# The second output product in two halves: the convolution's columns beside the recurrence's output stage

## The reference

```
y, ... = rwkv_bidir(...)                              # the recurrence
yn  = (y - mean) * rsqrt(var + eps) * gn_g + gn_b     # per head of 64
a_x = (yn + bonus) * (sigmoid(xg) @ g_up)
b_x = short_conv(px_cv, conv_w)
x   = x + g1 * (concatenate([a_x, b_x]) @ w_out)      # 1024 x 1024 weights
hx  = modulate(rmsnorm(x, norm2_g), sh2, sc2)
x   = x + g2 * expert_choice_ffn(hx, router_w, ...)
```

## Time and profile before

| | us |
|---|---|
| runs | 2788.32, 2792.85, 2795.87 |
| median | 2792.85 |
| the profiled execution | 2790.04 |
| its span in the trace | 2788.0 |
| recurrence's chunks | 1414 to 1907 |
| recurrence's output | 1908 to 1969 |
| output product with scores | 1969 to 2109 |
| TensorE busy, share of the span | 2370.7, 85% |
| VectorE busy, share of the span | 1687.5, 61% |

### The profile page before, as it was taken

How to read it: one execution, slowest core, us unless ns; L and a number is a source line. 1 busy time by engine, 2 the same in 40 slices (tenths; PEclk the granted TensorE clock), 3 DMA queues, 4 the chain that set the end, 5 groups by cost and what they waited for, 6 DMA issues and landing times. The chain is left out here.

```text
span 2788.0 us, 55283 instructions
## 1 busy us (share of the span) xinstructions
PE 2370.7 (85%) x23038; PEld 1852.1 (66%) x23038; DVE 1687.5 (61%) x2124; ACT 980.6 (35%) x1536; POOL 665.8 (24%) x672
## 2 busy tenths in 40 slices
PE   4998988899987599997858888888691799999994
PEld 2876755578866488886237777775481588888883
DVE  5981569421143655664645555553447899999994
ACT  3112532311032400000424333333220577777773
POOL 1321676123300123220045555440000000000000
PEclk8999999999998599997579999997795799999997
DMA  5331024411132453110321101101532599999994
GB/s 214 113 106 63 1 82 121 168 31 46 31 122 105 133 192 118 39 38 12 127 86 27 31 22 26 26 12 51 221 112 107 227 407 407 393 395 397 398 384 171
DMA packets 135851, 401.45 MB, mean 144 GB/s; under 512 B 55410, under 2 KB 65266, under 8 KB 108114
## 3 DMA queue, kind: packets, MB, share of 16 engines
q1 hardware_dynamic: 124692, 363.70, 35.1%
q0 software_dynamic: 4608, 16.78, 2.5%
q10 hardware_dynamic: 6336, 17.80, 1.7%
HBM read 342.64 MB, written 55.59 MB: 143 GB/s over the span
## 5 line engine op out<-in xcount | busy, mean ns | idle before, releaser
L3336 DVE TENSOR_TENSOR ex_wl<-ew_raw,ex_wh 128x2048 fp32r<-128x2048 f32 x192 | 435.4, 2289 | 41.9 <-ACT ex_wh L3298 38.3
L3298 ACT ACTIVATE ex_wh<-ew_raw 128x2048 fp32r<-128x2048 f32 x192 | 367.5, 1919 | 108.7 <-PE ex_U L3242 40.3
L130 PE MATMUL sp_acc<-b2h_hi,sp_wh 128*128 128x512 f32 (+1 forms) x528 | 194.8, 369 | 12.9 <-POOL sp_wl L1710 12.9
L130 PE MATMUL sp_acc<-b2h_lo,sp_wh 128*128 128x512 f32 (+1 forms) x528 | 194.4, 368 | 0.0
L130 PE MATMUL sp_acc<-b2h_hi,sp_wl 128*128 128x512 f32 (+1 forms) x528 | 194.3, 368 | 0.0
L3219 POOL DMA_INDIRECT x<-ex_o,ex_at x16 | 26.5, 1657 | 494.6 <-DVE ex_o L3359 494.6
L2361 DVE TENSOR_TENSOR rc_t<-rc_chain,b_level 128x256 f32<-128x256 f32 x200 | 84.5, 423 | 85.3 <-PE rc_chain L2459 83.5
L1708 POOL CAST sp_wh<-sp_w 128x1024 fp32r<-128x1024 f32 x26 | 27.8, 1069 | 409.4 <-DMA sp_w<-in_w_conv 233.5
L130 PEld LDWEIGHTS sp_acc<-b2h_hi,sp_wh 128*128 128x128 f32 x528 | 100.1, 190 | 30.6 <-POOL sp_wl L1710 13.3
L130 PEld LDWEIGHTS sp_acc<-b2h_hi,sp_wl 128*128 128x128 f32 x528 | 100.0, 189 | 16.6
L130 PEld LDWEIGHTS sp_acc<-b2h_lo,sp_wh 128*128 128x128 f32 x528 | 100.2, 190 | 16.3
(11 more groups left out here) (485 smaller groups left out, 6062.1 us busy)
## 6 DMA issues: line engine op xcount, KB each, us to landing
ew_raw<-in_exp_gate SPq DMA_DIRECT2D x64, 1024.0 KB, 7.8
ew_raw<-in_exp_up SPq DMA_DIRECT2D x64, 1024.0 KB, 8.9
ew_raw<-in_exp_down SPq DMA_DIRECT2D x64, 1024.0 KB, 7.4
b2p_pT<-in_ada_w SPq DMA_DIRECT2D x32, 512.0 KB, 6.2
rc_ac<-ac SPq DMA_DIRECT2D x40, 256.0 KB, 3.6
b_pj<-in_ada_w SPq DMA_DIRECT2D x8, 1024.0 KB, 11.9
ssm_wm<-in_w_merge SPq DMA_DIRECT2D x16, 512.0 KB, 3.6
ac<-rp_ac SPq DMA_DIRECT2D x4, 2048.0 KB, 7.2
```

The source lines that it names most:

```text
L130: ins = nc.tensor.matmul(out, w[a][:, k, :], h[b][:, k, cols], start=(first and n == 0), stop=(last and n == 2))
L3298: nc.scalar.activation(wh[:, n % RING], raw[:, n % RING], ACT.Copy).then_inc(q["w_hi"], 1)
L3336: V.tensor_tensor(wl[:, n % RING], raw[:, n % RING], wh[:, n % RING].bitcast(f32), ALU.subtract).then_inc(q["w_lo"], 1)
```

## The change

The rows 4 to 7 of w_out and the columns b_x are multiplied in the output stage of the recurrence, and their part is added to the residual on chip; the later stage multiplies only a_x, which stays in SBUF.

- `rwkv_chunks` gets a function `ahead`, by which SP loads w_out's rows 4 to 7 (512 KB each) before the loop.
- `rwkv_output` loads b_x (in four pairs of blocks), the row g1, the residual `xm` and w_out's rows 0 to 3. ScalarE and VectorE split the weights (`weight_high`, `weight_low`) and columns (`columns_high`, `columns_low`); TensorE has 16 units `product(b, h)` of 12 matmuls between its other work; ScalarE evacuates each unit, and GpSimd multiplies by g1 and adds to `xm`, two passes per block. The fan, the gate and the sums have one PSUM buffer each. The result is not stored. The split weights lie over the inputs of the recurrence.
- `out_scored` has four k instead of eight: 24 matmuls per block, scores before k = 1, transpositions before k = 3, no loads of weights, columns or residual. It stands inside the phase `b2p`, which owns semaphores now.
- The recorded offset of a tile is rounded up to 32 bytes.

```diff
@@ rwkv_chunks, SP
                 sp.dma_start(ka[:, 0], I["kcols"][:, 1, :]).then_inc(ka_loaded, 16)
+                ahead(sp)
@@ rwkv_output, GpSimd and SP
+                for b in range(NB):
+                    t = tmp[:, b % 2, :]
+                    pool.wait_ge(q["evacuated"], 2 * b + 2)
+                    nc.gpsimd.tensor_tensor(t, t, row[:], ALU.mult).then_inc(q["weighed"], 1)
+                    pool.wait_ge(q["weighed"], b + 1)
+                    pool.wait_ge(xm_loaded, 32)
+                    nc.gpsimd.tensor_tensor(xm[:, b, :], xm[:, b, :], t, ALU.add).then_inc(q["xm_ready"], 1)
...
-                    sp.dma_start(aT_dram[:, b, hs], bonus[:, b, hs]).then_inc(q["stored"], 16)
+                for i in range(4):
+                    sp.wait_ge(q["w_lo"], i + 1)
+                    sp.dma_start(ow[:, i, :], I["w_out2"][:, i, :]).then_inc(ow_loaded[i], 16)
@@ rwkv_output, TensorE (fanned(n) waits for scaled >= n, gated(n) for done >= n)
+                def product(b, h):
+                    u = 2 * b + h
+                    pe.wait_ge(q["s_lo"], b + 1)
+                    if u >= 3:
+                        pe.wait_ge(q["evacuated"], u - 2)
+                    for k in range(4):
+                        if u == 0:
+                            pe.wait_ge(q["w_lo"], k + 1)
+                        nc.tensor.matmul(prod[:, u % 3, :], sh[:, b % 2, k, :], wh[:, 4 + k, halves[h]], start=(k == 0), stop=False)
+                        nc.tensor.matmul(prod[:, u % 3, :], sh[:, b % 2, k, :], wl[:, 4 + k, halves[h]], start=False, stop=False)
+                        last = nc.tensor.matmul(prod[:, u % 3, :], sl[:, b % 2, k, :], wh[:, 4 + k, halves[h]], start=False, stop=(k == 3))
...
+                product(3, 0)
+                fanned(3)
+                gated(3)
+                summed(7)
+                product(3, 1)
                 turned(1)
                 for n in range(4, N):
+                    product(n // 2 + 2, n % 2)
                     fanned(n)
                     gated(n)
+                for b in (6, 7):
+                    for h in range(2):
+                        product(b, h)
@@ rwkv_output, ScalarE
+                for b in range(1, NB):
+                    if b + 1 < NB:
+                        columns_high(b + 1)
+                    evacuate(2 * b)
+                    if b == 1:
+                        unit(4)
+                    if b == 2:
+                        unit(6)
+                    evacuate(2 * b + 1)
...
+                    if b < HP:
+                        biased(b)
+                    if b == 3:
+                        rooted(1)
+                    if 2 <= b < 6:
+                        weight_high(2 + b)
@@ rwkv_output, VectorE
                 meaned(0)
...
+                output(1)
+                weight_low(4)
+                output(2)
+                columns_low(4)
+                output(3)
                 meaned(1)
+                weight_low(5)
+                columns_low(5)
+                weight_low(6)
+                output(4)
+                columns_low(6)
+                output(5)
+                weight_low(7)
+                columns_low(7)
+                output(6)
+                output(7)
@@ out_scored
+    KA = 4
...
-                    for k in range(KD):
-                        if k == 2 and b >= 2:
+                    for k in range(KA):
+                        if k == 1 and b >= 2:
                             scored(b - 2)
-                        if k == 6 and b >= 1:
+                        if k == 3 and b >= 1:
                             turned(b - 1)
...
-                    V.tensor_tensor(yb, yb, xt[:, s, :], ALU.add).then_inc(q["added"], 1)
+                    V.tensor_tensor(yb, yb, xm[:, b, :], ALU.add).then_inc(q["added"], 1)
```

More of the change, by code:

```diff
@@ L2625, in _, with rwkv_output @@
                 outputs(NCK, (NCK - 1) % 2)
-def rwkv_output(nc, T, I, pT, y, bonus_dram, bonus, aT_dram):
+def rwkv_output(nc, T, I, pT, y, bonus_dram, bonus, bx_dram, xmid, mod_dram, split, ow, ow_loaded, xm, row):
+    wh, wl = split
+    halves = [slice(0, 512), slice(512, 1024)]
     with Phase(nc, "ro") as ph:
@@ L2682, in turned @@
                     for i in range(4):
-                        last = nc.tensor.transpose(var[0:8, h, i * P:(i + 1) * P], inv[:, h, i * 8:(i + 1) * 8], T.ident[:])
+                        last = nc.tensor.transpose(var[0:8, i * P:(i + 1) * P], inv[:, h, i * 8:(i + 1) * 8], T.ident[:])
                     last.then_inc(q["turned"], 1)
[L2686 to L2691, removed]
                 def fanned(n):
@@ L2695, in fanned @@
                     pe.wait_ge(q["rows_ready"], h + 1)
-                    if n >= 2:
-                        pe.wait_ge(q["scaled"], n - 1)
-                    nc.tensor.matmul(fan[:, n % 2, :], heads[:, b, :], inv_rows[:, h, :], start=True, stop=True).then_inc(q["fanned"], 1)
+                    if n == 0:
+                        pe.wait_ge(q["loaded"], 48)
+                    else:
+                        pe.wait_ge(q["scaled"], n)
+                    nc.tensor.matmul(fan[:], heads[:, b, :], inv_rows[:, h, :], start=True, stop=True).then_inc(q["fanned"], 1)
@@ new lines, in gated @@
+                def gated(n):
+                    h, b = todo[n]
+                    if n:
+                        pe.wait_ge(q["done"], n)
+                    nc.tensor.matmul(gate[:], gup[:, b * P:(b + 1) * P], pT[:, XB, CTX + h * 512:CTX + (h + 1) * 512], start=True, stop=True).then_inc(q["gated"], 1)
+                def product(b, h):
[9 more added lines that the diff above has]
+                        last = nc.tensor.matmul(prod[:, u % 3, :], sl[:, b % 2, k, :], wh[:, 4 + k, halves[h]], start=False, stop=(k == 3))
+                    last.then_inc(q["product"], 1)
@@ L2701, in _ @@
                 pe.wait_ge(q["matrix"], 1)
                 centred(0)
[L2703 to L2706, removed]
+                centred(1)
+                summed(0)
+                centred(2)
+                summed(1)
+                product(0, 0)
+                centred(3)
+                summed(2)
+                product(0, 1)
+                summed(3)
+                product(1, 0)
@@ L2707, in _ @@
+                turned(0)
+                centred(4)
+                product(1, 1)
+                fanned(0)
                 gated(0)
+                summed(4)
+                centred(5)
+                product(2, 0)
+                fanned(1)
                 gated(1)
[L2709 to L2716, removed]
+                summed(5)
@@ L2717, in _ @@
+                centred(6)
+                product(2, 1)
+                fanned(2)
+                gated(2)
+                summed(6)
+                centred(7)
+                product(3, 0)
[3 more added lines that the diff above has]
+                product(3, 1)
                 turned(1)
                 for n in range(4, N):
+                    product(n // 2 + 2, n % 2)
                     fanned(n)
                     gated(n)
+                for b in (6, 7):
+                    for h in range(2):
+                        product(b, h)
@@ L2740, in biased @@
                         act.wait_ge(q["loaded"], 48)
-                    nc.scalar.activation(bonus[:, b, :], bonus[:, b, :], ACT.Identity, bias=cols[:, 1, b:b + 1]).then_inc(q["biased"], 1)
-                for n in range(4):
-                    unit(n)
-                biased(0)
[L2746 to L2751, removed]
+                    A(bonus[:, b, :], bonus[:, b, :], ACT.Identity, bias=cols[:, 1, b:b + 1]).then_inc(q["biased"], 1)
@@ new lines, in evacuate @@
+                def evacuate(u):
+                    b, h = u // 2, u % 2
+                    act.wait_ge(q["product"], u + 1)
+                    if b >= 2 and h == 0:
+                        act.wait_ge(q["xm_ready"], b - 1)
+                    A(tmp[:, b % 2, halves[h]], prod[:, u % 3, :], ACT.Copy).then_inc(q["evacuated"], 1)
+                weight_high(0)
+                unit(0)
+                weight_high(1)
+                columns_high(0)
+                unit(1)
+                weight_high(2)
```

184 lines of the change are left out of this document (98 added, 86 removed).

## The result

The changed kernel runs 2806.61 us (median, 2799.87 to 2809.83), beside 2793.24 for the kernel before: ratio 1.0042, 95% interval 1.0023 to 1.0061 (the ratio is estimated over all runs; that of the two medians is 1.0048). The profiled execution of the first comparison, 2799.87 us with a span of 2798.1, is the quickest of its four runs.

What follows compares the result with a forecast made beforehand. It took the product's stage as bound by TensorE, after 14 us of loading, and the output stage as holding little work. +47.7 - 48.5 + 4.5 + 3.1 + 0.9 = +7.7 gave 2797.7, as a median 2800; range 2782 to 2818.

Steps and rivals of the forecast that it cites:

- TensorE's work and its waits: Output stage: 74.9 us of TensorE work at full clock, plus waits from the new order, tail and stage change, 98.3.
- D: Output stage: fan 7, behind unit 11, waits for weight-low 7 and columns-low 7; 4.95 us.
- B: Output stage: second transposition waits for unit 7, its evacuation, a bias, a square root and reciprocal; 2.55 us.
- C: Output stage: fan 5 waits for output 4 behind weight-low 6, and gate 5 waits too; 4.35 us.
- The clock in the output stage: Half clock on TensorE after idle time, a little more than one stretch: 5 us, bounds 0 and 15.
- A: Output stage: fan 3 waits for output 2's scaling, which stands behind weight-low 4 on VectorE; 3.3 us.
- The product's stage: Later stage: no load in front, blocks 9.7 us apart on VectorE's chain; -48.5 us, and +4.5 for half clock.
- The chunk loop's start: Four weight rows issued in front of the loop's first transfers delay its start; +3.1 us, bounds 0 and 6.
- The extra barrier: Leaving the enclosing phase, which now owns semaphores, costs one more change of stage; +0.9 us.
- rival 2: Product's stage loses the clock in every block, at idle time before the transposes: 15 instead of 4.5, 2811; chance 0.17.
- 1: Rival: clock holds in both stages and GpSimd seldom meets VectorE on a path; 2780 to 2791, say 2786; chance 0.30.
- 3: Rival: output stage stays at half clock throughout; about +40, 2840; chance 0.08.

Runs made afterwards that it cites:

- the other order: The changed kernel with only the order of work on the engines altered, no work added or removed: 2765.52 us, ratio 0.9938 to the kernel before.
- The fillers: The changed kernel plus 24, 22 and 34 unread matmuls in three of TensorE's output-stage waits: ratio 1.0044 to the kernel before, stage 112.5 us.

## Why the prediction came out as it did

The time, 2806.61, lies in the range, 6.6 us above the forecast, and the sign is that of its sum. The result is in "slower" (0.40), not in "same" (0.38), which the forecast itself was in. That the number is so near is in part luck: the output stage took 121 us where 105 to 112 were forecast, for the cost of TensorE's clock there was mis-sized, about 16 us where 5 were taken, and errors of the other sign made up for most of it. By its steps:

- **TensorE's work and its waits**: the waits right as a sum, the work 2 us short. The matmuls of a unit start 0.233 us apart here; I had divided a window of 2.00 us by the nine that began in it, 0.222. From its first matmul at 1905.61 to the pause before 2027.88, TensorE waits 0.72 + 2.37 + 5.13 + 4.94 + 0.69 + 7.69 = 21.5 us; the terms were 1.5 + 3.3 + 2.55 + 4.35 + 4.95 = 16.65, and 5 for GpSimd, 21.65. The run without GpSimd's passes divides them: it waits 15.5 us, so 6 are GpSimd's. (The 4.95 of D does not follow from its parts: 3.85 and 0.7 are 4.55.) Each wait is where it was put. B was mis-worked: I let the second root wait for the bias of block 3 alone, but output 3's last two operations stand in between. The first of them waits for that bias and then meets GpSimd, the first row here; the others are the hit splits of C and D (timeline of VectorE):

```profile
1964.21 1.83 DVE L2892 TENSOR_TENSOR b2p_y<-b2p_y,b2p_bonus 128x512 f32<-128x512 f32 x1 [9.46 <-ACT b2p_bonus L2815]
...
1979.56 2.53 DVE L2900 TENSOR_TENSOR b2p_o_lo<-b2p_ow,b2p_o_hi 128x1024 fp32r<-128x1024 f32 x1 [8.52 <-ACT b2p_o_hi L2820]
...
1997.74 2.53 DVE L2900 TENSOR_TENSOR b2p_o_lo<-b2p_ow,b2p_o_hi 128x1024 fp32r<-128x1024 f32 x1 [9.25 <-ACT b2p_o_hi L2820]
2000.20 2.82 DVE L2904 TENSOR_TENSOR ro_sl<-ro_bt,ro_sh 128x512 fp32r<-128x512 f32 x1
```

The two weight splits take 2.53 instead of 1.22 and columns-low 7 takes 2.82, where six of the eight splits of columns in this stage took 0.67 to 0.69. The rule of the Trainium skill, page "SBUF — State Buffer", section "Who interferes with whom", which the prediction weighed, holds in these rows: operations with two inputs in SBUF are hit, while the scalings, whose other input is in PSUM, stay at 0.75 at most.
- **The clock in the output stage**: the step that failed, in size. I took 5 us, "a little more than one such stretch", with 15 as the upper bound, and looked at C and D alone, although A and B stood on my own list at 3.3 and 2.55 us, both longer than the 1.84 us that had cost the clock before. TensorE was busy 92.8 us [first table]. In the other order it did the same work in 78.4 us, the first 3 of them at half clock, which makes some 77 us at full clock, so the clock cost some 16: a stretch at half clock behind each of A to D, 25 us busy and so 12.5 lost, and one at the start. The fillers took 6.0 of it away while the waits stayed, and the new order took both away: 121.2 - 85.6 = 35.6 us, of which 21.2 are waits and the other 14.4 clock.
- **The product's stage**: right, and better than the term for the clock. The first block's output begins 9.9 us after the stage's first transfer (forecast 9.6), the last one's 78.1 after it (forecast 77.5 + 4.5), and blocks from the third on are 9.51 apart (forecast 9.7). Timeline of VectorE, the first step of three blocks, and of PE, the transpositions of one:

```profile
2056.97 1.22 DVE L3068 TENSOR_TENSOR o_y<-o_acc,b2p_row 128x1024 f32<-128x1024 f32 x1 [1.98 <-PE o_acc L3010]
...
2066.49 1.22 DVE L3068 TENSOR_TENSOR o_y<-o_acc,b2p_row 128x1024 f32<-128x1024 f32 x1 [1.98 <-PE o_acc L3010]
...
2104.54 1.22 DVE L3068 TENSOR_TENSOR o_y<-o_acc,b2p_row 128x1024 f32<-128x1024 f32 x1 [2.58 <-PE o_acc L3010]
```

```profile
2054.45 1.10 PE L2984 MATMUL o_pt<-all_ident,o_xn 128*128 128x128 f32 x8 [1.10 <-DVE o_xn L3081]
```

The 1.10 us of idle time before the transpositions were as foreseen and cost no clock, so rival 2 did not come; only the 2.99 us in block 1 were followed by half clock, which made that block 11.1 us.
- **The chunk loop's start**: mechanism right, size too small. GpSimd's first use waits 5.83 us for the transfer, and TensorE starts 22.5 us after the stage's first transfer instead of 16.8 (forecast 3.1 more). Timeline of GpSimd and PE in the changed kernel, where that transfer is at 1410.34, then PE in the kernel before, where it is at 1414.29:

```profile
1420.42 0.72 POOL L2235 TENSOR_TENSOR rc_bst<-b2k_nkk,rc_ac 128x256 f32<-128x256 f32 x1 [5.83 <-DMA rc_ac<-ac]
...
1432.86 0.70 PE L2460 MATMUL rc_chain<-rc_bst,rc_ar 64*64 64x64 f32 x16 [27.29 <-POOL rc_ar L2259]
```

```profile
1431.04 0.70 PE L2459 MATMUL rc_chain<-rc_bst,rc_ar 64*64 64x64 f32 x16 [21.51 <-POOL rc_ar L2258]
```

Putting the rows behind the loads made the loop 4.0 us shorter in one pair of profiles and 5.7 in the other. That the whole loop is only 1.1 us longer than before is the clock of two single executions, as far as the rows show it. Behind the first matmuls the kernel before was at half clock until about 1443, the changed one only until about 1436, which gave some 2.9 us back (15 us further on its matmuls are 2.9 us late instead of 5.8); and the kernel before had a dip later that the changed one lacks. PE alone, the kernel before (three rows), then the changed one:

```profile
1437.00:1443.00 6.00, 5.98 (x128) 0.50 0.02 4
1790.00:1800.00 10.00, 7.61 (x240) 0.91 0.25 56
1800.00:1810.00 10.00, 8.80 (x317) 0.92 0.01 3
```

```profile
1437.00:1440.00 3.00, 2.49 (x84) 1.00 0.01 3
```

The loop varies from one profile to the next anyway: 493.1 to 495.2 us in six with the rows in front, beside 490.9 and 488.2 with the rows behind, so the 1.1 by itself says little.
- **The extra barrier**: 1.26 instead of 0.92 on the path, less than the 0.9 added:

```profile
2119.37 0.28 DVE L3224 TENSOR_REDUCE rt_per_token<-all_scores 128x8 f32<-128x128 f32 x1 [1.26 <-PEq L89]
```

Against the sum's +7.7, the profiled execution is +10.1 by its spans: 12.6 more in the output stage, 4.5 less in the product's stage with its barrier, 2.0 less in the chunk loop, and 3.7 less in stages that the change does not touch. The rest of the distance is that the median lies 6.7 us above the profiled execution, where 2.8 was taken. Of the rivals, 1 and 2 did not happen, and 3 happened in part: 16 us lost are some 32 us at half clock, a quarter of the stage.

## What to carry to other kernels

Work that is moved into a stage to fill its idle time must not be put in front of the stage's own chain on the engines that feed it: here the same instructions gave +0.4% to +0.7% in one order and -0.6% in another. When TensorE has pauses, price what follows them too: in this stage each wait of 2.4 to 7.7 us was followed by 4 to 10 us at half clock, and together these cost 12.5 us on top of 20.8 us of waiting. And where a saved load looks like the gain, check what the early load delays: a few rows in front of a queue cost 4 to 6 us at the start of another stage.

## What was unexpected

The 2.50 us pause at the stage's start did not fix what the clock does: 1.00 behind it in the kernel before, in the changed one about 0.5 only from 1911, and 0.50 at once in the kernel with the later weight rows. What TensorE did in front of it was the same loop each time. This stays open; in six profiles with the same order up to fan 2, that fan came 35.9 to 39.5 us after the stage's first transfer, so it moves the stage by some 3.5 us.
